# Norms by token with root and reciprocal on 2 to 8 columns; first branch's scores as one matmul of 96 rows, second branch's key zero-padded

## What is computed

```python
def rms_norm(x, g):
    y = xf * lax.rsqrt(jnp.mean(xf * xf, axis=-1, keepdims=True) + EPS)
    return (y * g.astype(jnp.float32)).astype(x.dtype)

# branch a (mla): 8 heads, 64 channels without and 32 with rotation,
# the rotated key k_pe is one for all heads
q = concatenate([q[..., :64], rope(q[..., 64:], cos, sin)], axis=-1)
k = concatenate([kv[..., :64], broadcast_to(k_pe, (B, S, 8, 32))], axis=-1)
s = einsum('bqhd,bkhd->bhqk', qb, k) * (64 + 32) ** -0.5

# branch b (swa): 8 query heads of 64 channels on 2 key heads
s = einsum('bnqgrd,bnkgd->bngrqk', q, kb) * 64 ** -0.5
```

## Time and profile before

| | us |
|---|---|
| median of 3 runs | 2265.28 (2263.27 to 2267.95) |
| the profiled execution | 2264.3 |
| its span in the profile | 2262.5 |
| TensorE busy | 2177.0 (96%) |
| VectorE busy | 1644.7 (73%) |
| ScalarE busy | 1289.9 (57%) |
| GpSimd busy | 20.7 (1%) |

### The profile page before, as it was taken

One profiled execution on the slowest core, in us unless ns is written; L12 is line 12 of the kernel. 1 busy time (PEld: TensorE's weight loads), 2 busy tenths in 40 slices (PEclk: granted clock), 3 DMA queues, 4 the chain that ended last, 5 costly groups with the idle time before them and its releaser, 6 DMA issues.

```text
span 2262.5 us, 33030 instructions
## 1 busy us (share of the span) xinstructions
PE 2177.0 (96%) x12694; PEld 1878.3 (83%) x12694; DVE 1644.7 (73%) x1930; ACT 1289.9 (57%) x1546; POOL 20.7 (1%) x13
## 2 busy tenths in 40 slices
PE   6999999999999999999898999999999999999997
PEld 6897788997788888999796888888888887888886
DVE  6556766655756775555664888888888988888896
ACT  2544433454442474434643677777777777777775
POOL 0000000000000120000000000000000000000000
PEclk6999999999999999999999999999999999999999
DMA  9684445455333533555427999999999999999990
GB/s 283 185 267 144 131 145 135 115 180 156 114 112 114 167 127 98 183 186 169 136 78 260 345 373 326 367 333 362 342 354 349 348 372 328 372 331 368 330 363 35
DMA packets 348651, 536.39 MB, mean 237 GB/s; under 512 B 51084, under 2 KB 195392, under 8 KB 348552
## 3 DMA queue, kind: packets, MB, share of 16 engines
q1 hardware_dynamic: 342992, 530.81, 68.5%
q10 hardware_dynamic: 5560, 4.19, 0.6%
HBM read 533.89 MB, written 1.07 MB: 236 GB/s over the span
## 4 chain that ended last, share of the span: by engine, by line
PE 73%; DVE 4%; ACT 3%; issue 1%; DVEq 0%; ACTq 0%
PE bank L651 21%; PE bank L653 20%; PE bank L652 20%; PE bank L620 3%; PE bank L1244 1%; ACT w_hi L1872 1%; PE bank L1193 1%; PE bank L1291 1%; PE bank L809 1%; DVE w_lo L2646 1%; DVE piece_lo L2282 1%; DVE rstd L1993 1%; ACT piece_hi L1394 1%; PE bank L791 0%; PE bank L628 0%
## 5 line engine op out<-in xcount | busy, mean ns | idle before, releaser
L2646 DVE TENSOR_TENSOR w_lo<-pool,w_hi 128x2048 fp32r<-128x2048 f32 x336 | 764.4, 2291 | 110.4 <-ACT w_hi L1872 110.0
L1872 ACT ACTIVATE w_hi<-pool 128x2048 fp32r<-128x2048 f32 x336 | 643.3, 1917 | 141.0 <-PE bank L653 140.9
L651 PE MATMUL bank<-w_hi,xe_hi 128*128 128x512 f32 x896 | 358.0, 400 | 12.8 <-DVE w_lo L2646 8.9
L653 PE MATMUL bank<-w_hi,xe_lo 128*128 128x512 f32 x896 | 350.2, 391 | 0.0
L652 PE MATMUL bank<-w_lo,xe_hi 128*128 128x512 f32 x896 | 349.8, 390 | 0.0
L651 PE MATMUL bank<-h_upper,upper 128*128 128x256 f32 x992 | 291.5, 294 | 4.9 <-DVE h_lo L2110 3.2
L652 PE MATMUL bank<-h_lo,upper 128*128 128x256 f32 x992 | 282.6, 285 | 0.0
L653 PE MATMUL bank<-h_upper,ring_lo 128*128 128x256 f32 x992 | 282.5, 285 | 0.0
L2020 DVE TENSOR_TENSOR ring_lo<-ring,upper 128x1024 fp32r<-128x1024 f32 x132 | 160.5, 1222 | 101.6 <-ACT upper L1405 101.3
L2282 DVE TENSOR_TENSOR piece_lo<-ring,piece_hi 128x1024 fp32r<-128x1024 f32 x118 | 145.1, 1237 | 109.0 <-ACT piece_hi L1394 108.8
L651 PEld LDWEIGHTS bank<-w_hi,xe_hi 128*128 128x128 f32 x896 | 168.6, 188 | 57.2 <-DVE w_lo L2646 17.2
(11 more groups left out here) (386 smaller groups left out, 3455.3 us busy)
## 6 DMA issues: line engine op xcount, KB each, us to landing
pool<-in_od_exp_w SPq DMA_DIRECT2D x336, 1024.0 KB, 7.1
ring<-in_w_in SPq DMA_DIRECT2D x52, 1024.0 KB, 5.3
ring<-in_ev_ffn_w SPq DMA_DIRECT2D x33, 1024.0 KB, 5.3
ring<-in_w_ada SPq DMA_DIRECT2D x24, 1024.0 KB, 7.9
ring<-in_od_w_in SPq DMA_DIRECT2D x12, 1024.0 KB, 6.4
ring<-in_ev_w_in SPq DMA_DIRECT2D x10, 1024.0 KB, 5.3
ring<-in_w_out SPq DMA_DIRECT2D x8, 1024.0 KB, 5.1
ring<-in_w_in SPq DMA_DIRECT2D x16, 256.0 KB, 5.1
```

What stands on the lines that cost most here:

```text
L651: nc.tensor.matmul(b, left[0], right[0], start=first, stop=False, skip_group_check=True)
L653: return nc.tensor.matmul(b, left[1], right[0], start=False, stop=last, skip_group_check=True)
L1872: nc.scalar.activation(w_hi[q % 3], ring_slot(q), ACT.Copy)\
L2646: V.tensor_tensor(w_lo[q % 3], ring_slot(q), w_hi[q % 3].bitcast(F32), ALU.subtract).then_inc(item_vector, tick(item_vector, "lo", q))
```

## The change

Norms: all but pre of layer 0 and the q and kv norms sum their squares by token. The squares are the stationary operand, one column of 1/n the moving one, so a bank holds one value a token on the partitions, in 2 to 8 columns. Root and reciprocal work on those columns (`rtok`). `spread` then multiplies a column of `rtok`, repeated over 128 columns, with the identity, and so puts the value of each token on all partitions again, in a bank that VectorE reads as the factor. It is a step of TensorE that waits for VectorE. In mix 1 and ffn 1 it stands directly behind the squares, in ffn 0 behind `clear_sums`, in pre, post and mix 0 behind `keep_busy(4)`.

Scores: the query's rotated 32 rows are written under the 64 plain ones of each head, the key's rotated rows are copied under those of each head, and branch a takes one matmul of 96 rows for each block of tokens. Branch b's key is held twice, with zeros in the other half, and the matmul takes 128 rows. Some tiles move for this (flip, the halves of the query and key), and the waits follow.

```diff
+        def token_square(b, at, tile, k, scale, start, stop):
+            for t in range(NT):
+                m = nc.tensor.matmul(b[:, at + t:at + t + 1], tile[:, k, P * t:P * t + P], mean[scale][:, 0:1],
+                                     start=start and t == 0, stop=stop, skip_group_check=True)
+            return m
+
+        def token_squares(key):
+            b = claim("gemm", ("ms", *key), rstd_ready, *key)
+            for k in range(KD):
+                pe.wait_ge(sq_ready, when(sq_ready, *key, k))
+                m = token_square(b, 0, sq, k, 1024, k == 0, k == KD - 1)
+            m.then_inc(psum_ready, wrote("ms", *key))
+
+        def spread(key, first, n, freed_by, *step):
+
+            pe.wait_ge(rstd_ready, when(rstd_ready, *key))
+            b = claim("gemm", ("r", *key, first), freed_by, *step)
+            for t in range(n):
+                m = nc.tensor.matmul(b[:, P * t:P * t + P], rtok[:, first + t:first + t + 1].broadcast_to([P, P]), ident,
+                                     start=True, stop=True)
+            m.then_inc(psum_ready, wrote("r", *key, first))
...
                 if br == "a":
-                    nc.tensor.matmul(s, qn[r, i // 2, tok], kn[r, i // 2], start=True, stop=False)
-                    r = slice(ROPE * (i % 4), ROPE * (i % 4) + ROPE)
-                    m = nc.tensor.matmul(s, qr[r, i // 4, tok], krope[r, :], start=False, stop=True,
-                                         tile_position=(r.start, 0))
+                    m = nc.tensor.matmul(s, q_full(i)[0:HEAD + ROPE, tok], k_full(i)[0:HEAD + ROPE], start=True, stop=True)
                 elif br == "b":
-                    r = slice(HEAD * (i // 4), HEAD * (i // 4) + HEAD)
-                    m = nc.tensor.matmul(s, qb[r, i % 4, tok], kb[r, :], start=True, stop=True)
+                    m = nc.tensor.matmul(s, qb[:, i % 4, tok], kb_half(i // 4), start=True, stop=True)
...
-                mean_square(("pre", l), KD, 1024)
-                keep_busy(14)
+                token_squares(("pre", l))
+                keep_busy(4)
+                spread(("pre", l), 0, NT, h_ready, "pre", l, KD - 1)
+                keep_busy(6)
...
+            b = claim("gemm", ("ms", "sub", l), rstd_ready, "sub", l)
             for i in range(4):
-                b = claim("gemm", ("ms", "sub", l, i), rstd_ready, "sub", l, i)
                 pe.wait_ge(sq_ready, when(sq_ready, "sub", l, i, 0))
-                nc.tensor.matmul(b[:, 0:S], mean[128], subsq[:, i], start=True, stop=True)\
-                    .then_inc(psum_ready, wrote("ms", "sub", l, i))
+                m = token_square(b, 2 * i, subsq, i, 128, i == 0, True)
+            m.then_inc(psum_ready, wrote("ms", "sub", l))
             for c in range(2, KD):
                 branch_out("b", l, c)
+                if c in (3, 4):
+                    spread(("sub", l), 4 * (c - 3), 4, dve_step, "sub", l, 2 * (c - 3) + 1)
...
-            keep_busy(22)
-
-
-        mean_square(("mix", 0), KD, 1024)
-        keep_busy(12)
+            keep_busy(4)
+            spread(("post", l), 0, NT, dve_step, "yo", l, KD - 2)
+            keep_busy(12)
+
+
+        token_squares(("mix", 0))
+        keep_busy(4)
+        spread(("mix", 0), 0, NT, h_ready, "mix", 0, KD - 1)
+        keep_busy(5)
...
         clear_sums()
+        spread(("ffn", 0), 0, NT, h_ready, "ffn", 0, KD - 1)
...
-        mean_square(("mix", 1), KD, 1024)
+        token_squares(("mix", 1))
+        spread(("mix", 1), 0, NT, h_ready, "mix", 1, KD - 1)
...
+        def head_squares(p):
+            b = claim("gemm", ("ms", "gla", p), rstd_ready, "gla", p)
...
+        head_squares(0)
         head_outputs(2)
+        spread(("gla", 0), 0, 4, dve_step, "gla", 1)
         head_outputs(3)
         gate_piece(4)
         gate_piece(5)
-        for hd in range(2, 4):
-            mean_square(("gla", hd), 2, 256, first=2 * hd)
+        head_squares(1)
         gate_piece(6)
+        spread(("gla", 1), 4, 4, dve_step, "gla", 3)
         gate_piece(7)
...
+        def token_root(*key, first=0, n=NT):
+            b = psum(act, "ms", *key)
+            nc.scalar.activation(rtok[:, first:first + n], b[:, 0:n], ACT.Sqrt, bias=eps)\
+                .then_inc(root_ready, tick(root_ready, *key))
...
+            def two_heads(name, c, dst):
+                b = psum(act, name, l, c)
+                nc.scalar.activation(dst(2 * c)[0:HEAD], b[0:HEAD, 0:S], ACT.Copy)
+                nc.scalar.activation(dst(2 * c + 1)[0:HEAD], b[HEAD:P, 0:S], ACT.Copy)\
+                    .then_inc(proj_ready, tick(proj_ready, name, l, c))
...
+            act.wait_ge(rope_ready, when(rope_ready, "k", l))
+            every = krope[HEAD:HEAD + ROPE].unsqueeze(1).broadcast_to([ROPE, 4, S])
+            nc.scalar.activation(kn[HEAD:HEAD + ROPE], every, ACT.Copy)
+            nc.scalar.activation(gates[HEAD:HEAD + ROPE, 20:24], every, ACT.Copy)\
+                .then_inc(proj_ready, tick(proj_ready, "krows", l))
             for n in range(2):
                 form_behind(("qb1", l), n)
...
             for c in range(2):
-                rotate(("rotq", l, c), qr[:, c], "q", l, c)
+                b = psum(dve, "rotq", l, c)
+                V.tensor_tensor(tmp[:, 0], b[:, 0:S], sin, ALU.mult)
+                link(V.tensor_tensor(qrope[:, c], qrope[:, c], cos, ALU.mult))
+                for j in range(4):
+                    r = slice(ROPE * j, ROPE * j + ROPE)
+                    V.tensor_tensor(q_full(4 * c + j)[HEAD:HEAD + ROPE], qrope[r, c], tmp[r, 0], ALU.add)\
+                        .then_inc(rope_ready, tick(rope_ready, "q", l, 4 * c + j))
+                dve.wait_ge(rope_ready, when(rope_ready, "q", l, 4 * c + 3))
...
+            dve.wait_ge(proj_ready, when(proj_ready, "va", l, NT - 1))
+            V.memset(kb_half(0)[HEAD:P], 0.0)
+            V.memset(kb_half(1)[0:HEAD], 0.0).then_inc(kb_cleared, tick(kb_cleared, l))
...
-                if c in (1, 3):
-                    sub_norm(c - 1)
-                    sub_norm(c)
+                if c == 1:
+                    inverse_tokens("sub", l, n=8)
+                if c in (3, 4):
+                    sub_norm(2 * c - 6)
+                    sub_norm(2 * c - 5)
```

More of the change, by code:

```diff
@@ L1198, in _ @@
         mean_square_part(("ffn", 1), KD - 1, "attn")
+        spread(("ffn", 1), 0, NT, h_ready, "ffn", 1, KD - 1)
         w = take("router")
@@ L1603, in _ @@
                 modulation(1, 1)
-            for c in range(4):
-                root("sub", l, c, slot=c)
+            token_root("sub", l, n=8)
             for n in range(PIECES):
@@ L1620, in _ @@
                     form_behind(("out", l, c // 2), c % 2)
-            root("post", l)
+            token_root("post", l)
             form_behind(("out", l, 3), 1)
@@ L1627, in _ @@
             piece_upper(n)
-        root("mix", 0)
+        token_root("mix", 0)
         pair_uppers(("mix", 0))
@@ L1732, in _ @@
                 behind=lambda k: piece_upper(EVOUT + k + PIECES))
-        root("ffn", 0)
+        token_root("ffn", 0)
         pair_uppers(("ffn", 0))
@@ L1825, in _ @@
         gate_out(3)
-        root("gla", 0, slot=0)
-        root("gla", 1, slot=1)
+        token_root("gla", 0, n=4)
         head_out(2)
@@ L1831, in _ @@
         gate_out(5)
-        root("gla", 2, slot=2)
-        root("gla", 3, slot=3)
+        token_root("gla", 1, first=4, n=4)
         gate_out(6)
```

83 lines of the change are left out of this document (57 added, 26 removed).

## The result

The changed kernel takes 2243.8 us (median of 4, 2239.5 to 2244.0) beside 2264.3 for the kernel before: ratio 0.990, 95% interval 0.989 to 0.992. Run once more later it took 2241.3 beside 2264.2 (0.991, 0.989 to 0.992). The profiled execution took 2244.0, its span is 2242.2 where before's is 2262.5: 20.3 less. The forecast was 2235, 30 less, in a range of 2221 to 2248. The gain came, two thirds of it.

What follows compares the result with a forecast made beforehand. TensorE's issue was taken as the bound, around norms a ScalarE and VectorE chain. Terms -28.7 - 9.8 - 6.0 + 1.7 + 2.0 + 6.5 + 1.0 + 3.0 = -30.3 gave 2235 us from 2265.3; range 2221 to 2248.

Steps and rivals of the forecast that it cites:

- Branch a: First branch's scores: four 96-row instructions instead of eight save 1.62 us a unit, 26.0 over 16 units.
- The transfer wait: Branch a units: ScalarE's wait for a weight tile delays the turned probabilities, +1.0 us (0 to 4).
- Rivals 1, 4 and 5: Branch a: other engines pace units, 2248 (0.14); 96 rows priced as 64 plus 32, 2261 (0.04); gaps lower clock, 2301 (0.04).
- Branch b: Second branch's scores: the zero-padded key turns 1.05 us into 0.88 a unit, saving 2.7 over 16 units.
- Sub-norms: Squared sums to third branch's last output: 27.8 us instead of 32.7, saving 9.8 over both layers.
- Norms on the path: Post twice, pre 1, mix 0, mix 1, ffn 1: chain of 1.3 us instead of 2.36, together -6.0.
- ffn 0: The spread stands behind clear_sums on TensorE's queue, so the multiply comes later: +1.7 us.
- GLA: GLA head norms: reciprocals are hidden, so only two spreads and the squares count, +2.0 us (0 to 2.3).
- Clock: One-column squares at pre 1, mix 0, mix 1 bring half clock; +1 us each, +3.0 (0 to 10).
- Rival 3: At every norm the half clock holds for two stretches: +10 instead of +3, 2242 to 2246; chance 0.08.
- Ahead of the units: Rotation adds and key-row copies before the attention units: +4.2 us in layer 0, +2.3 in layer 1, together +6.5.
- Rival 2: Additions before the units vanish in layer 0's transfer wait and 32-row adds overlap: 2227 us; chance 0.12.

Runs made afterwards that it cites:

- c2: c1 with the second branch's scores on the 64 rows again instead of the zero-padded 128: 2224.5 us.
- c1: Changed kernel with 128-column squares except sub-norms, ffn 0 spread before clear_sums, rotation bank freed early, key rows copied later, branch b normalise before statistics: 2221.5 us.
- w1: Changed kernel, but the squared sums of pre 1, mix 0 and mix 1 multiply with 128 equal columns instead of one: 2238.0 us.
- f1: Changed kernel with the spread of ffn 0 ahead of clear_sums on TensorE's queue, not behind it: 2239.7 us.
- the second run: The changed kernel timed once more with no edit, as the measure for kernels on the same chip: 2241.3 us.
- r1: Changed kernel, but a rotation's bank is freed once its product with the sine is read, not after the last add: 2234.6 us.
- k1: Changed kernel, but ScalarE copies the key's rotated rows behind the copies of kb and vbt, not ahead of the bias tables: 2240.5 us.

## Why the prediction was right or wrong, point by point

**Branch a: right.** 1.62 a unit was forecast, (54.45 - 41.57)/8 = 1.61 was measured in layer 0 with its wait, 1.69 in layer 1. 96 rows cost what 128 cost. The transfer wait was priced +1.0 and cost 0.5. Rivals 1, 4 and 5 fell with this: most units come at 5.38, the clock stays at 1.00 in them, and one unit waits.

**Branch b: the size was right, but it did not become time.** 0.17 a unit was forecast and c2 beside c1 shows 0.20. But the step took it that a TensorE instruction less is time less, and in branch b it wasn't: the 5.73 of a unit were already set by VectorE's chain of bias, statistics and normalise, so the saving became a wait of 0.18. The trace of before could have told: the statistics of a unit can't start before its scores, and the transposes hang behind them in VectorE's order. I had read VectorE's busy time, not its order.

The rule of the Trainium skill that spoke against the padding (page "TensorEngine Tiling (Array Packing)", Performance Considerations: contractions of up to 64 rows are meant for row tiling) was priced in the prediction as if the 64 rows were the faster form. The runs show the opposite for the form used here, 45.42 against 43.85. The page's gain is for tiles that run side by side, and in these kernels both matmuls of a unit take the same rows one after the other, so no run here tests that.

**Sub-norms: right.** Forecast 27.8 from squares to last output, measured 27.9; -9.9 in the changed kernel and -10.4 alone.

**Norms on the path: half right.** At post of layer 0 the root starts at 386.86 and the first multiply at 388.31, 1.45 where 2.36 was the earlier trace rows: forecast 1.3.

```profile
386.86 0.26 ACT L1479 ACTIVATE small<-bank,small 128x2 f32<-128x2 f32 x1 [0.93 <-PE bank L646]
...
387.22 0.17 DVE L2071 RECIPROCAL small<-small 128x2 f32<-128x2 f32 x1 [2.13 <-ACT small L1479]
...
388.31 1.28 DVE L2363 TENSOR_TENSOR pool<-pool,bank 128x512 f32<-128x512 f32 x2 [0.91 <-PE bank L662]
```

The hand-over from reciprocal to multiply is 0.92 (387.39 to 388.31), not 0.8. At mix 1 the same step takes 2.35 before (1087.50 to 1089.85), 1.83 in the changed kernel at half clock and 1.32 in w1, so there too the step was sized rightly and the clock took half of it. But the gain of 1.0 was applied to six norms, and at mix 0 most of it isn't there. The prediction took off a tenth for VectorE coming late; in fact VectorE comes to the reciprocal 3.3 us after the root is done, and in the trace of before it was 3.1 (752.23 to 755.34), which could have been read:

```profile
724.25 0.24 ACT L1479 ACTIVATE small<-bank,small 128x2 f32<-128x2 f32 x1
...
727.81 0.16 DVE L2071 RECIPROCAL small<-small 128x2 f32<-128x2 f32 x1
...
729.04 2.34 PE L671 MATMUL bank<-ident,mean 128*128 128x128 f32 x10
729.34 1.28 DVE L2394 TENSOR_TENSOR h<-h,bank 128x512 f32<-128x512 f32 x2 [1.37 <-PE bank L662]
...
731.17 4.05 PE L633 MATMUL bank<-h,pool 128*128 128x256 f32 x11
```

The prediction also said that the shorter keep_busy only fills what is left, and that was wrong there: its ten instructions, at half clock, run until 731.2, and the first product comes 1.8 after the multiply where it came 0.8 after it before. I tried no kernel with fewer of them; this is read, not tested. At pre 1 a piece of VectorE (L2098, 395.21 to 396.43) stands ahead of the reciprocal, so that the reciprocal starts 0.7 after the root is done at 395.61.

**ffn 0: right**, +1.9 for +1.7, and by the mechanism named, as f1 shows.

**GLA: right but for the clock.** The head norms cost +2.0 in five traces (the second run, f1, r1, c1, c2: 52.75 and 52.76 against 50.78), as forecast, and +3.6 in those where the clock falls among them, as in this stage of the changed kernel (clock 0.91; at the same place before, 1.00):

```profile
1144.00:1164.00 20.00, 20.00 (x162) 20.00 (x161) 6.60 (x16) 10.31 (x15) 0.00 (x0) 0.91 0.01 2
```

**Clock: the mechanism right, the place and size of it off.** +1 at each of three norms was forecast. It cost nearly nothing at pre 1 (0.5, by w1) and mix 0, and 3.3 at mix 1 (1.4 to 3.4 over all traces). There the squares take 6.96 instead of 5.38, and the half clock holds on through the thin first product and the start of the projections; that TensorE has no other work between is read, not tested. The term also left out every other place. Behind the new waits ahead of the units the half clock costs 3.1 more (see "Ahead of the units"), among GLA's heads 1.6. Rival 3 (half clock for two stretches at every norm, +10 for +3, 2242 to 2246) had the measured time and nearly the size: from the query projection to the first expert TensorE is at 0.50 for 61.4 us in the changed kernel's trace and for 37.5 before. The 24 us more are, by an estimate that halves them, at most 12 us of time. Its places were wrong, as pre 1 and mix 0 cost next to nothing. Of the 10 us that are missing, some 5.5 are the clock's by the stretches.

The Trainium skill, page "TensorE: Matmul & The Clock Gate", section "What's actually happening", lets the clock follow how busy the engine has been. For one-column work these traces don't agree as far as busy means what the profile counts: 32 instructions of one column and 32 of 128 columns both fill the engine, and only the latter bring the clock back early (0.81 against 0.53 over 18 us).

**Ahead of the units: wrong by 4.8**, the largest miss: +11.3 for +6.5. The larger part of it is a term that was put at nothing: the clock behind the new waits. In both layers the granted clock falls to 0.50 within 1 us of the end of the second wait (98.3 and 99.3 in layer 0). What follows takes 1.7 longer up to the end of the tables in layer 0, and 1.4 longer up to the next projection in layer 1. Of eight traces with these waits seven have the fall in layer 1 (the stretch is 79.0 to 80.5); k1 hasn't it and takes 77.6, and r1, c1 and c2, without the waits for the adds, take 75.5 against 74.65 before. The waits themselves were priced too low. The adds of 32 rows come 0.45 apart like full ones (1.76 for four), where "overlapped ones less" had been assumed, so each of the two rotations holds its bank 1.35 longer, not 1.0: TensorE waits 1.35 and 1.89 instead of 0 and 0.55, in both layers, and 0.49 more for ScalarE's copy of the query. That is 3.1 a layer where 1.9 and 2.3 had been forecast. ScalarE's part (2.0 for the big copies in layer 0) was sized about rightly, k1 gives 2.1 for it, some 0.5 of which is the clock's. Rival 2 is refuted: nothing of these additions vanishes in layer 0's wait for a transfer (the stretch from the tables' end to the first unit is 73.3 for 72.8).

**The sum.** The misses are +4.8 ahead of the units, +2.3 in branch b, +1.6 in GLA and +3.2 at mix 1 and behind it, less 1.4 in the units of branch a and 0.8 at the end; with the small rest (+0.9 at post and mix 0, -0.5 elsewhere) they make the 10 between -30.3 and -20.3. Misses of both signs are in it: the units of branch a and the end gave 2.2 more than forecast. The time lies 4 us inside the range because the range took in the clock's 10 and rival 1's 12.8, not because the terms were right.

## What to carry to other kernels

A saving on the busiest engine is time only if no other engine's order ties the loop to the old pace: look in which order the helper engine does the old unit's and the new unit's work, not at its busy share alone. Before lengthening the tail of an operation that reads a PSUM bank, give the bank back at its last reader, and put a wait on TensorE's queue ahead of, not behind, work that nobody needs yet. A reduction on TensorE that needs one column may as well take 128 where it fills a gap: it cost no more here, and less time at half clock followed. And price a new wait on TensorE together with the clock that may fall behind it: in layer 1, 3.1 us of waits were followed by another 1.4 at half clock in one run of the changed kernel, by 2.8 in its second, and by nothing in k1.

## What the runs showed of the hardware

- Four matmul instructions of 256 columns in 32-bit floats hold TensorE for 1.06 us with 64 rows of contraction and for 0.78 with 96 or 128 (with the different first gap behind them: 0.20 a unit between 64 and 128).
- One-column instructions of the squares come 0.11 us apart at full clock and 0.21 at half clock (32 in 6.96 us); in w1 the 128-column ones of the same operands come 0.11 and 0.21 apart too (32 in 6.22 us, 5.1 of them at half clock). The one column saves nothing.
- Around the squares of mix 1 the granted clock is at 0.50 for 13.7 to 17.1 us at a stretch in the eight traces with one-column squares, and for 6.8 in the three with 128-column ones.
- A reciprocal of 2 to 8 columns takes 0.15 to 0.20, of 256 columns 1.75. Adds on 32 partitions cost VectorE what 128 do: 0.45 each.
- Copies of half the partitions, 64 x 256, take ScalarE 0.38 and come 0.39 apart, the time of a whole 128 x 256 one (0.38).
- The places at which the granted clock falls outside such stretches differ between executions of one kernel, and move single stretches by 1.5 to 3 us.
